# Token mixer: a mask product in two pieces, four low halves on GpSimd, and another order on VectorE and TensorE

## What is computed

```python
h = rms_norm(x, norm1_g) * (1 + sc1) + sh1
y = token_mixer(h, hc, ...)          # mLSTM heads and gated linear attention, both directions
x = x + g1 * y
h2 = rms_norm(x, norm2_g) * (1 + sc2) + sh2
x = x + g2 * peer_ffn(h2, ...)       # 128 expert rows a token, gathered from HBM

# in the token mixer
d_log = where(causal, b_t - b_s + i_s, NEG)              # the mask
num = (q k^T * exp(d_log - m)) @ v + inter * (C q)
ml = sigmoid(ml_o) * head_rms(ml_h, ml_g)
gl = silu(gla_r) * head_rms(gla_h, gla_g)
y = concat([ml, gl]) @ w_out
```

## Time and profile before

| | us |
|---|---|
| median of 3 runs | 1903.7 (1903.67 to 1903.73) |
| the profiled execution | 1902.06 |
| its span | 1900.3 |
| TensorE busy | 1774.5 (93%) |
| VectorE busy | 1338.1 (70%) |
| ScalarE busy | 842.2 (44%) |
| GpSimd busy | 300.5 (16%) |

### The profile page before, as it was taken

One profiled execution on the slowest core, in us unless ns is written; L12 is line 12 of the kernel. 1 busy time (PEld: TensorE's weight loads), 2 busy tenths in 40 slices (PEclk: granted clock), 3 DMA queues, 4 the chain that ended last, 5 costly groups with the idle time before them and its releaser, 6 DMA issues.

```text
span 1900.3 us, 26516 instructions
## 1 busy us (share of the span) xinstructions
PE 1774.5 (93%) x10506; PEld 1396.4 (73%) x10506; DVE 1338.1 (70%) x2632; ACT 842.2 (44%) x1604; POOL 300.5 (16%) x341
## 2 busy tenths in 40 slices
PE   9999999999999999999999999999999787777777
PEld 8999997999999999979999899865555332232222
DVE  7676677777677766777777698877775567575745
ACT  6334557543353335575343664534533233332323
POOL 0000211000000002200000000033444433333330
PEclk9999999999999999999999999999999999999999
DMA  9675542677557754437675442599999999999997
GB/s 320 216 242 190 192 162 85 208 240 259 176 191 238 261 180 155 162 103 248 216 243 172 95 134 95 192 386 421 421 421 421 421 421 421 421 422 421 421 421 292
DMA packets 196868, 508.66 MB, mean 268 GB/s; under 512 B 10419, under 2 KB 142855, under 8 KB 160008
## 3 DMA queue, kind: packets, MB, share of 16 engines
q1 hardware_dynamic: 159592, 238.51, 37.8%
q0 software_dynamic: 37152, 268.45, 34.0%
HBM read 505.87 MB, written 1.06 MB: 267 GB/s over the span
## 4 chain that ended last, share of the span: by engine, by line
PE 67%; DMA 21%; DVE 7%; ACT 3%; issue 1%; SPq 0%; POOL 0%; DVEq 0%; ACTq 0%; POOLq 0%
DMA RAW<-in_c_experts,BIG 14%; PE PB L322 13%; PE PB L323 12%; PE PB L324 12%; PE PB L2802 7%; PE PB L635 4%; PE PB L637 4%; PE PB L636 4%; DMA BIG<-in_c_experts,BIG 3%; DMA HIF<-in_c_experts,BIG 2%; PE PB L2724 2%; PE PB L1124 1%; DMA HTF<-in_c_experts,BIG 1%; DVE LOWS L280 1%; PE PB L1164 1%
## 5 line engine op out<-in xcount | busy, mean ns | idle before, releaser
L280 DVE TENSOR_TENSOR LOWS<-RAW,HIGH 128x2048 fp32r<-128x2048 f32 (+2 forms) x130 | 298.7, 2306 | 43.1 <-ACT HIGH L268 42.6
L322 PE MATMUL PB<-HTR,HIGH 128*128 128x256 f32 (+1 forms) x1072 | 306.7, 286 | 0.4 <-DVE LOWS L280 0.2
L323 PE MATMUL PB<-HTR,HIGH 128*128 128x256 f32 (+1 forms) x1072 | 305.9, 285 | 0.0
L324 PE MATMUL PB<-HTR,LOWS 128*128 128x256 f32 (+1 forms) x1072 | 305.2, 285 | 0.0
L268 ACT ACTIVATE HIGH<-RAW 128x2048 fp32r<-128x2048 f32 (+3 forms) x138 | 264.8, 1923 | 78.1 <-DMA RAW<-in_ffn_w_gate 30.7
L322 PEld LDWEIGHTS PB<-HTR,HIGH 128*128 128x128 f32 x1072 | 203.0, 189 | 5.9 <-DVE LOWS L280 0.7
L323 PEld LDWEIGHTS PB<-HTR,HIGH 128*128 128x128 f32 x1072 | 201.1, 188 | 4.4
L324 PEld LDWEIGHTS PB<-HTR,LOWS 128*128 128x128 f32 x1072 | 201.4, 188 | 2.1
L3161 ACT ACTIVATE BIG<-BIG 128x2 f32<-128x2 f32 (+1 forms) x132 | 26.8, 203 | 372.2 <-DVE BIG L3066 372.2
L2802 PE MATMUL PB<-RAW,BIG 128*128 128x512 f32 x296 | 145.5, 621 | 43.9 <-ACT BIG L3172 43.9
L825 ACT ACTIVATE BIG<-BIG 128x256 f32<-128x256 f32 x88 | 36.7, 417 | 315.4 <-DVE BIG L742 315.4
(11 more groups left out here) (482 smaller groups left out, 4036.3 us busy)
## 6 DMA issues: line engine op xcount, KB each, us to landing
RAW<-in_ffn_w_up SPq DMA_DIRECT2D x32, 1024.0 KB, 6.5
RAW<-in_ffn_w_down SPq DMA_DIRECT2D x32, 1024.0 KB, 5.1
RAW<-in_ffn_w_gate SPq DMA_DIRECT2D x31, 1024.0 KB, 5.6
RAW<-in_w_in SPq DMA_DIRECT2D x22, 1120.0 KB, 5.8
RAW<-in_c_wmod SPq DMA_DIRECT2D x20, 1024.0 KB, 4.9
BIG<-in_ffn_w_gate SPq DMA_DIRECT2D x12, 1024.0 KB, 6.5
BIG<-in_ffn_w_up SPq DMA_DIRECT2D x12, 1024.0 KB, 9.0
BIG<-in_ffn_w_down SPq DMA_DIRECT2D x12, 1024.0 KB, 5.0
```

What stands on the lines that cost most here:

```text
L280: e.tensor_tensor(u.l, u.raw, u.h.bitcast(F32), ALU.subtract).then_inc(*low_done.up())
L322: e.matmul(o, lh, rh, start=k == 0, stop=False)
L323: e.matmul(o, lh, rl, start=False, stop=False)
L324: last = e.matmul(o, ll, rh, start=False, stop=k == len(ls) - 1)
```

## The change

In `decay`, the mask product of 2 x 256 columns is issued as two products of 256. In the mixer's VectorE queue, the two low halves of the second output weight each move one step back. GpSimd makes the low halves of the third and fourth output weight, four pieces in all, behind its memset, each as soon as the high half of its tile is there; VectorE no longer makes them. TensorE waits for GpSimd's count (`pool_low`, which starts at 2) where it waited for VectorE's. In the output, VectorE scales block 0 ahead of gating block 1, ScalarE takes block 0's root ahead of squaring block 1, and TensorE turns block 0 ahead of the fourth weight's first piece instead of behind it.

```diff
--- before.py
+++ after.py
@@ -1641,8 +1641,9 @@
                     e.wait_ge(*read_of(last_in[2]))
                     e.wait_ge(*mask_done.next())
                 e.matmul(PB[2][:, :], ONES[:, :], DGM.rearrange("p h t -> p (h t)"), start=True, stop=False)
-                e.matmul(PB[2][:, :].rearrange("p (i n) -> p i n", i=2), IDENTR, MASKR[d], start=False,
-                         stop=True).then_inc(*decay_full.up())
+                for i in range(2):
+                    x = e.matmul(PB[2][:, i * 256:(i + 1) * 256], IDENTR, MASKR[d][:, i, :], start=False, stop=i == 1)
+                x.then_inc(*decay_full.up())
 
             def scores(n):
                 d, c = OUTS[n]
@@ -2075,12 +2076,12 @@
             weights(2)
             decays(3)
             evacuate(e, "V", "GR10")
-            low_half(e, SECOND["out"][1], 0)
             output(2)
             weights(3)
-            low_half(e, SECOND["out"][1], 1)
+            low_half(e, SECOND["out"][1], 0)
             output(3)
             evacuate(e, "V", "GR11")
+            low_half(e, SECOND["out"][1], 1)
 
         def mixer_scalar(e):
             squares_scalar(e, PIECES_FFN, x_done, X_AFTER["ffn3"] - 4, M_HN)
@@ -2222,6 +2223,7 @@
         CHUNKS = [[4, 5, 6, 7, 0, 1, 2, 3], [7, 6, 5, 4, 3, 2, 1, 0]]
 
         squares, oo_done, gated = sig("squares"), sig("oo_done"), sig("hg_done")
+        pool_low, POOL_BEFORE = kc_done, 2
         MOD_ROWS = nc.dram_tensor("mod_rows", (2, 1024), F32, kind="Internal").ap()
 
         OO = BIG[:, AT_K + 2048:AT_K + 4096].rearrange("p (b n) -> p b n", b=2)
@@ -2367,7 +2369,6 @@
             masked(0)
             e.wait_ge(*squares.next())
             mean_squares(e, TT, R8[:, 0:8])
-            low_half(e, SECOND["out"][2], 0)
             update(4)
             masked(1)
             e.wait_ge(*rs_done.next())
@@ -2401,6 +2402,12 @@
 
             e.wait_ge(intra_full.sem, 8)
             e.memset(AT_PLACE, 0.0).then_inc(*bias_masked.up())
+            for t in SECOND["out"][2:4]:
+                e.wait_ge(high_done.sem, t.splits)
+                for x in range(2):
+                    q = slice(4 * x, 4 * x + 4)
+                    e.tensor_tensor(t.l[:, q, :], t.raw[:, q, :], t.h[:, q, :].bitcast(F32),
+                                    ALU.subtract).then_inc(*pool_low.up())
 
 
 
@@ -2491,15 +2498,12 @@
             e.wait_ge(*gated.next())
             e.wait_ge(carry_read.sem, 8)
             gate(0)
-            low_half(e, SECOND["out"][2], 1)
             means(0)
-            low_half(e, SECOND["out"][3], 0)
+            scale(0)
             gate(1)
-            scale(0)
             means(1)
             lower(0)
             scale(1)
-            low_half(e, SECOND["out"][3], 1)
             e.wait_ge(mixer_in.sem, 192)
             mix_update(e, 0, 0)
             lower(1)
@@ -2527,8 +2531,8 @@
 
             e.wait_ge(carry_read.sem, 8)
             square(0)
+            sqrt_scalar(e, R8[:, 8:12])
             square(1)
-            sqrt_scalar(e, R8[:, 8:12])
             raise_(0)
             sqrt_scalar(e, R8[:, 12:16])
             raise_(1)
@@ -2548,17 +2552,18 @@
 
             e.wait_ge(carried.sem, 8)
             for j in range(4):
-                if j < 3:
+                if j < 2:
                     tile_ready(e, SECOND["out"][j])
                 else:
-                    e.wait_ge(first_low.sem, 6)
+                    e.wait_ge(pool_low.sem, POOL_BEFORE + j)
+                if j == 3:
+                    gla_turn(0)
                 if j == 0:
                     for k in range(4):
                         e.wait_ge(ht_low.sem, 8 * turn_count["p"] + k + 1)
                         part(0, j, k, k + 1)
                 else:
                     part(0, j, 0, 4)
-            gla_turn(0)
             for j in range(4):
                 if j == 0:
                     for k in range(4, 8):
@@ -2568,7 +2573,7 @@
                     gla_turn(1)
                 else:
                     if j == 3:
-                        tile_ready(e, SECOND["out"][j])
+                        e.wait_ge(pool_low.sem, POOL_BEFORE + 4)
                     part(0, j, 4, 8).then_inc(*out_done.up())
             e.wait_ge(ot_low.sem, OT_BEFORE + 8)
             e.wait_ge(x_done.sem, X_MIX + 3)
```

## The result

The changed kernel takes 1905.93 us (median of 22 runs, 1905.23 to 1907.88), the kernel before 1902.93 in the same comparison (22 runs, 1901.83 to 1904.61): the ratio is 1.0017, 95% interval 1.0011 to 1.0023. That is 3.0 us slower: under 0.2% of the time, but the interval, 2.1 to 4.4 us, does not reach zero. The profiled execution took 1905.26 us, its span is 1903.5.

What follows compares the result with a forecast made beforehand. TensorE was taken to bound 1190 to 1242 us, ahead of GpSimd's first gather, and the DMA engines the rest. Terms 0 + 0 + 2.6 - 1.2 = 1.4 us slower, on 1903.7, gave 1905.1 us; range 1902.3 to 1907.4.

Steps and rivals of the forecast that it cites:

- the four L1938: In VectorE's queue ahead of the masks: all four run 1195.67 to 1196.81, GpSimd's first low half follows, to 1199.15.
- the first rival: Ahead of the masks, GpSimd gets in between the four L1938: 3.8 us lost, 2.6 net, 1906.3 us; chance 0.25.
- Mask product: In decay, two products of 256 columns instead of one of 512: taken as 0, at most 1.0 us added.
- The second weight's halves: VectorE's low half moved from ahead of output(2): gain under 0.1 us, taken as 0.
- One low half on GpSimd: GpSimd's time for one low half of 1024 elements: 2.34 us, bounds 2.2 and 3.0.
- The collision: GpSimd's first two halves hold up VectorE's steps with two SBUF operands: own(0) 2.6 us late, 2.3 to 3.9.
- three signs: Low half behind L1585 at 2 us or more; L2364 held up; TensorE idle 2 to 3 us ahead of own(0).
- The fourth weight's halves hit nothing: Ahead of the output's scales, GpSimd's last two halves meet no VectorE step with two SBUF operands: no loss.
- slower beyond 3.8 us: GpSimd's third half between L2376's two pieces: 3.4 us slower with the forecast, 4.6 with the first rival (1908.3); chance 0.08.
- The turn and scale(0): In the output, the turn ahead of the fourth weight and an earlier scale(0) gain 1.2 us, bounds 0.8 and 1.5.
- 0.84 + 0.25: At the output's first turn: 0.84 us of TensorE idle saved, plus 0.25 of the turn's 0.66 that next products overlap.
- 0.1 of small waits that the low halves made: In the output: the part of the turn's gain from waits made by VectorE's low halves, 0.1 us.

Runs made afterwards that it cites:

- kernel 8: The kernel before with only the mask product in two pieces and the second output weight's two low halves moved later: 1902.34 us, ratio 0.9997.
- kernel 4: The change with 24 idle transposes on TensorE in its wait for L1939, into a bank zeroed behind them: 1904.41 us.
- kernel 2: The change with GpSimd's low halves held until the last L1939 is done: 1909.75 us, and 1909.09 us when run once more.
- kernel 6: The kernel before with only the output's new order, all low halves staying on VectorE: 1902.35 us, ratio 0.9998.
- kernel 1: The change with GpSimd's four low halves held until VectorE has the first batch's masks: 1901.12 us, ratio 0.9991.
- kernel 10: The change with the third weight's first half back on VectorE, GpSimd starting after the fourth high half, its last half held until scale(0): 1900.78 us.
- kernel 3: The change with GpSimd held until the last L1939 and the fourth weight's low halves held until L2377 is done: 1903.76 us, ratio 1.0005.
- kernels 5: The change with each of GpSimd's four low halves cut into four instructions of 256 elements: 1902.23 us, ratio 0.9999.

## Why the prediction was right, and where it was wrong

That the change would be slower, by less than 3.8 us, held, and so did the range: 1905.93 was measured in 1902.3 to 1907.4, and the forecast was 1905.1. The loss was forecast at 1.4 us and came as 3.0; the median of before fell from 1903.7 to 1902.93 with more runs, which brought 1905.1 nearer by luck. The step that failed is "the four L1938 (two SBUF operands) run from 1195.67 to 1196.81; GpSimd's first half gets in behind them". What happened is the first rival, and TensorE's clock behind it.

- **Mask product, 0:** right; a pair takes 0.80 us, as the one product did.
- **The second weight's halves, 0, under 0.1 gained:** right, 0.05 in kernel 8.
- **One low half on GpSimd, 2.34 us:** 2.37 (4.73 for two). The bound in proportion to the row of 640, 2.47, and the estimate of 2.25 were farther off.
- **The collision, 2.6 us:** 4.84. That VectorE's steps with two operands in SBUF and GpSimd's halves shut each other out was right, from one pair of rows. The order was not: GpSimd's first half followed its memset without the pause that I had put there and was 0.02 us ahead of the first of the four. The first rival let it in behind the first of them, priced at 3.8, and had three of them pass before the second half; one passed. The added wait is 5.38 - 1.14 = 4.24, of which 3.48 reach own(0) in kernel 4, whose clock stays up. None of the three signs that I named behind L1939 came (the low half at over 2 us, L2366 held up, TensorE idle ahead of own(0)): they belong to the order of kernel 2, where all three are seen and 2.26 us are lost, just under the range's 2.3. The rule of the Trainium skill (page "SBUF — State Buffer", section "SBUF: two separate sides"), that whoever starts first holds the shared pair for its whole instruction, is borne out by 2.51 and 2.43 us for two of the four, and by 3.09 for all four once GpSimd's instructions are short; I named it for the rival and gave the rival less than the forecast.
- **What the sum left out:** TensorE's clock. A wait was priced as its length; 1.58 us of the 4.84 is added to the work behind it, most of it at 1.2 GHz; kernel 4 wins back 1.36.
- **The fourth weight's halves hit nothing:** right here, by 0.6 us (L2377's second piece starts at 1213.3, GpSimd at 1213.93). The rival "slower beyond 3.8 us" has the right mechanism, and kernel 2 shows what it costs.
- **The turn and scale(0), 1.2 us:** 2.08. The gap behind the turn gave 1.15, where I had put 0.84 + 0.25. The rest was mis-sized: "0.1 of small waits that the low halves made" is 0.8, as the 120 products around the two turns take 14.46 us instead of 15.27 (from the first product to the lookup's first step, less the time from each turn's start to the next product). That scale(0) is early only without the low halves is shown by kernel 6.

The two errors have opposite signs, 2.24 too little loss and 0.88 too little gain, so the number came out better than its parts; that is luck.

## What to carry to other kernels

Before work moves to GpSimd, list which of VectorE's steps in that stretch have two operands in SBUF, and give GpSimd its start by a wait on a step of VectorE behind which only work on PSUM follows. Look at small steps from SBUF to SBUF too: L2419 in kernel 1 and L2420 in kernel 10, of eight and four columns, were caught. In a string of short steps each pays a whole GpSimd instruction as long as GpSimd has a next one, so if they must overlap, short instructions on GpSimd cost less. Price a wait of TensorE as long as those here, 2.2 to 3.1 us, with work at half clock behind it as a possibility, and look for the next place where a step that is late by a us meets something that it used to pass. Edits that make room for each other, here an order and a freer engine, are priced together, not one by one.

## What was not expected of the hardware

- TensorE's clock fell to 1.2 GHz after waits of 3.14 and 2.98 us, and after waits of 2.24 and 2.23 us it stayed in one execution and fell in another of the same kernel (in kernel 3 it stayed after 2.25). So one program had times of 1903 and of 1909 us. In the change it fell when the work had begun again: the granted clock is 1.00 in the wait, 0.92 in 1202 to 1203, and 0.50 in 1203 to 1206.
- A VectorE instruction with one operand in SBUF can be caught as well: L2419 of eight columns took 1.32 us beside GpSimd's half, while a reduction from SBUF, L2417, kept its 1.21. The same step for one block was caught in kernels 5 (L2418, 0.50 us) and 10 (L2420, 0.99). By the Trainium skill (page "SBUF — State Buffer", section "SBUF: two separate sides") VectorE also takes the shared pair in a mode that uses two ports; the trace does not show the mode of L2419, so this stays a reading.
